# A hybrid encoder layer on one core: filler matmuls around the first transposes and in the choice of tokens are taken out

## What is computed

```python
def hybrid_layer(x, ...):
    h = rmsnorm(x, norm1_g)                       # first step: scale rows, then project
    z = jnp.einsum('bld,dc->blc', h, w_in) + b_in
    ...
    x = x + (g_a * y_a + g_b * y_b) @ w_o
    x = x + expert_choice_moe(rmsnorm(x, norm2_g), router_w, exp_w_gate, exp_w_up, exp_w_down)

def expert_choice_moe(h, router_w, w_gate, w_up, w_down):
    logits = (tok @ router_w).astype(jnp.float32)
    aff = jax.nn.softmax(logits, axis=-1)
    gate, idx = lax.top_k(aff.T, cap)             # cap = 64 tokens per expert and sequence
    xs = tok[idx]                                 # gather
    hid = silu(einsum('ecd,edf->ecf', xs, w_gate)) * einsum('ecd,edf->ecf', xs, w_up)
    ye = einsum('ecf,efd->ecd', hid, w_down) * gate[..., None]
    out = zeros_like(tok).at[idx.reshape(-1)].add(ye.reshape(-1, D))
```

## Time and profile before

| | before |
|---|---|
| median of the runs | 1494.81 us (3 runs, 1494.58 to 1495.61) |
| profiled execution | 1495.38 us, its span 1493.6 us |
| mean granted TensorE clock | 0.994 |
| TensorE busy | 1468.4 us (98%) |
| VectorE, ScalarE, GpSimd busy | 1186.9, 817.8, 163.1 us |

### The profile page before, as it was taken

How to read it: one execution, slowest core, us unless ns; L and a number is a source line. 1 busy time by engine, 2 the same in 40 slices (tenths; PEclk the granted TensorE clock), 3 DMA queues, 4 the chain that set the end, 5 groups by cost and what they waited for, 6 DMA issues and landing times.

```text
span 1493.6 us, 18852 instructions
## 1 busy us (share of the span) xinstructions
PE 1468.4 (98%) x7018; PEld 1234.5 (83%) x7018; DVE 1186.9 (79%) x1016; ACT 817.8 (55%) x771; POOL 163.1 (11%) x119
## 2 busy tenths in 40 slices
PE   9999999999999999998999999999999999999996
PEld 8778888878788888887888888888888888888884
DVE  5688988896667766346888888888888888889896
ACT  6322232223622222333677777778777777777775
POOL 1000001000005200011010111011110112101101
PEclk9999999999999999999999999999999999999998
DMA  7110322533263255677999999999999999999997
GB/s 235 57 43 8 85 77 81 215 93 92 94 226 123 90 180 197 225 252 282 345 363 371 376 377 374 384 374 377 374 372 386 377 375 374 384 375 376 374 360 272
DMA packets 220972, 388.26 MB, mean 260 GB/s; under 512 B 8604, under 2 KB 87772, under 8 KB 220413
## 3 DMA queue, kind: packets, MB, share of 16 engines
q1 hardware_dynamic: 213692, 361.39, 68.2%
q0 software_dynamic: 7232, 26.22, 5.9%
HBM read 348.78 MB, written 38.80 MB: 259 GB/s over the span
## 4 chain that ended last, share of the span: by engine, by line
PE 90%; DVE 6%; DMA 1%; issue 1%; ACT 1%; SPq 0%; POOLq 0%; POOL 0%; DVEq 0%; ACTq 0%
PE ps L1724 29%; PE ps L1726 28%; PE ps L1725 28%; DVE conv_sum L1219 3%; PE ps L2086 1%; DMA w_raw<-in_w_in 1%; PE ps L2078 1%; PE ps L1764 1%; PE ps L2007 1%; DVE w_lo L1185 0%; PE ps L2025 0%; DVE expert_lo L1185 0%; DVE final_rows L1693 0%; PE ps L1731 0%; DVE top_index L1597 0%
## 5 line engine op out<-in xcount | busy, mean ns | idle before, releaser
L1185 DVE TENSOR_TENSOR expert_lo<-expert_raw,expert_hi 128x2048 fp32r<-128x2048 f32 (+1 forms) x285 | 598.5, 2114 | 93.1 <-ACT expert_hi L798 92.1
L798 ACT ACTIVATE expert_hi<-expert_raw 128x2048 fp32r<-128x2048 f32 (+1 forms) x285 | 506.5, 1778 | 177.7 <-PE ps L1726 173.9
L1724 PE MATMUL ps<-expert_hi,slot_tokens_T_hi 128*128 128x512 f32 (+1 forms) x768 | 289.7, 377 | 2.1 <-DVE slot_tokens_T_lo L1185 1.3
L1726 PE MATMUL ps<-expert_hi,slot_tokens_T_lo 128*128 128x512 f32 (+1 forms) x768 | 285.2, 371 | 0.0
L1725 PE MATMUL ps<-expert_lo,slot_tokens_T_hi 128*128 128x512 f32 (+1 forms) x768 | 285.1, 371 | 0.0
L1724 PE MATMUL ps<-hT_hi,w_hi 128*128 128x512 f32 x576 | 227.0, 394 | 1.0 <-DVE hT_lo L1197 1.0
L1726 PE MATMUL ps<-hT_hi,w_lo 128*128 128x512 f32 x576 | 224.3, 389 | 0.0
L1725 PE MATMUL ps<-hT_lo,w_hi 128*128 128x512 f32 x576 | 224.2, 389 | 0.0
L1724 PEld LDWEIGHTS ps<-expert_hi,slot_tokens_T_hi 128*128 128x128 f32 x768 | 144.2, 188 | 25.2 <-issue 3.8
L1726 PEld LDWEIGHTS ps<-expert_hi,slot_tokens_T_lo 128*128 128x128 f32 x768 | 144.2, 188 | 20.4
L1219 DVE SCALAR_TENSOR_TENSOR conv_sum<-a_padded,small_params,conv_sum 128x1024 f32<-128x1024 f32 x120 | 158.1, 1317 | 3.4
(11 more groups left out here) (300 smaller groups left out, 1844.5 us busy)
## 6 DMA issues: line engine op xcount, KB each, us to landing
expert_raw<-in_w_gate SPq DMA_DIRECT2D x64, 1024.0 KB, 8.7
expert_raw<-in_w_up SPq DMA_DIRECT2D x64, 1024.0 KB, 10.1
expert_raw<-in_w_down SPq DMA_DIRECT2D x64, 1024.0 KB, 8.1
expert_raw<-in_w_gate SPq DMA_DIRECT2D x32, 768.0 KB, 7.5
expert_raw<-in_w_up SPq DMA_DIRECT2D x32, 768.0 KB, 6.9
expert_raw<-in_w_down SPq DMA_DIRECT2D x32, 768.0 KB, 8.6
w_raw<-in_w_in SPq DMA_DIRECT2D x36, 512.0 KB, 4.8
gate_in<-gate_spill SPq DMA_DIRECT2D x22, 512.0 KB, 3.8
```

What stands on the lines that cost most here:

```text
L798: nc.scalar.activation(out, src, ACT.Copy, **scale).then_inc(s, 1)
L1185: V.tensor_tensor(out, src, high_part.bitcast(F32), ALU.subtract).then_inc(s, 1)
L1724: nc.tensor.matmul(out, a[0], b[0], start=first, stop=False)
L1726: return nc.tensor.matmul(out, a[1], b[0], start=False, stop=last)
```

## The change

Two helpers and their five calls are taken out of TensorE's program: `warm_up` with 26, 2 and 2 matmuls and the wait for `ones_set` ahead of it, and `keep_busy` with 48 and 22 matmuls. That is 100 matmuls. Nothing else in the kernel is touched; ONES stays, since the layer norm of the convolution branch multiplies by it.

```diff
-            def warm_up(n):
-
-                for _ in range(n):
-                    nc.tensor.matmul(PS[:, XT_BANK[KD - 1], (LT - 1) * P:LT * P], ONES[:], ONES[:], start=True, stop=True)
-
-            pe.wait_ge(ones_set, 1)
-            warm_up(26)
             for t in range(LT):
                 pe.wait_ge(scaled, t + 1)
                 for g in range(KD):
                     mm = x_tile_T(g, t)
                     if t == LT - 1:
                         mm.then_inc(xT_ready, 1)
-                if t < 2:
-                    warm_up(2)
@@
-            def keep_busy(n):
-
-                for _ in range(n):
-                    nc.tensor.matmul(PS[:, 2, 0:P], ONES[:], IDENT, start=True, stop=True)
-
             pe.wait_ge(aff_ready, 1)
             for t in range(HN):
                 mm = nc.tensor.transpose(PS[:, 3, t * P:(t + 1) * P], AFFW[:, t, :], IDENT)
             mm.then_inc(affT_mm, 1)
-            keep_busy(48)
             pe.wait_ge(pair_ready, 1)
@@
-            keep_busy(22)
             tokens_of(0)
             pe.wait_ge(pair_ready, 3)
             pe_body(0, 0, True, False)
```

## The result

The changed kernel takes 1498.49 us (median of 12 runs, 1496.60 to 1499.24), the kernel before on the same chip 1495.51 us (12 runs, 1494.58 to 1496.63): a ratio of 1.0017 with a 95% interval of 1.0010 to 1.0024, so +1.5 to +3.6 us, +3.0 us by the medians. The sign is settled; by size it lies at the 0.2% that I had named as the border of what can be told. The range held it, the forecast of +5.9 us is twice too large.

What follows compares the result with a forecast made beforehand. TensorE, busy in 98% of the span, was taken as the bound, so its losses come out at the end: start +3.6 and middle +2.3 make +5.9 us on 1494.81 us, 1500.7 us, range 1497.1 to 1502.5 us.

Steps and rivals of the forecast that it cites:

- at most some 0.05 us: Fillers' own delay ahead of each of three tiles and the gather's transposes; gain 0 to 0.2 us, taken as 0.
- Rival D: Fillers are on the path and the start's clock is full; 1494.6 or 1497.0 us by the middle's case; chance 0.05.
- clock column's 1.00: At the start, read as no record before the first change; clock taken as half until about 4.7 us.
- The start, forecast +3.6 us: Start without its fillers: late transposes 1.6, cold products 2.3, less 0.3 us for a wait at 20 us.
- The term of the cold products (+2.3 us): Products of x at the start run first at half clock, costing +2.3 us (1.85 to 2.8).
- the late transposes (+1.6 us): Start's transposes of x at half clock, 0.22 us each, make tile 3's first one, and the first product, 1.6 us late.
- Rival B: Transposes lift the clock too: start only +0.9 to +1.6 us, in all 2.6 to 4.6 us; chance 0.33.
- The 1.7 us wait takes nothing up: TensorE's longest wait before 690 us, for VectorE, moves along with TensorE's own z blocks and absorbs no loss.
- The two terms of -0.3 us: The 0.3 us waits at 20 us and for expert_lo in the last stretch each take 0.3 us back.
- The middle, forecast +2.3 us: Choice of tokens and experts: slower transposes +0.3, experts' cold products +2.3, less 0.3 us for the expert_lo wait.
- The slower transposes ahead of them: Slot and gather transposes at half clock, mostly hidden by VectorE's two splits: +0.3 us (0.1 to 0.5).
- upper end of 4.4 us for the start: Top of the start's range in the sum of 4.9 to 7.4 us, beside the middle's 3.0 us.

Runs made afterwards that it cites:

- middle_late: Kernel before with 20 more fillers ahead of the transposes of the first gathered tokens (keep_busy(42) for keep_busy(22)): 1501.29 us, ratio 1.0039.
- transposes_fill: Kernel before with the 70 filler matmuls in the choice of tokens replaced by 140 transposes: 1495.69 against 1495.71 us, ratio 1.0002.
- start_late: Kernel before with 20 more fillers ahead of the first transposes (warm_up(46) for warm_up(26)): 1501.79 us, ratio 1.0035.
- start_late_again: Repeat of the kernel before with warm_up(46) for warm_up(26), 20 more fillers at the start: 1501.61 us, ratio 1.0039.
- no_start: Kernel before without the 30 fillers at the start, the 70 in the choice of tokens kept: 1495.94 against 1496.05 us, ratio 1.0000.
- no_middle: Kernel before without the 70 fillers in the choice of tokens, the 30 at the start kept: 1498.05 us, ratio 1.0015.
- after: The changed kernel, all 100 fillers out, against the kernel before: 1498.49 against 1495.51 us, ratio 1.0017; its profiled execution took 1497.52 us.
- after_again: The changed kernel once more, the second series, against the kernel before on the same chip: 1497.62 against 1495.38 us, ratio 1.0013.
- only_48: Kernel before with keep_busy(22) taken out, keep_busy(48) and the fillers at the start kept: 1498.49 us, ratio 1.0018.
- count_only: Kernel before with keep_busy(48) replaced by 44 fillers and 24 small matmuls of 8 columns: 1504.16 us, ratio 1.0050.

## Why the prediction was right, and where its sum was not

**The path.** That taking the fillers out saves nothing of the 7.80 us that the chain of waits puts down to them was right: with the 52 records gone, the first transposes still start when VectorE has scaled the first tile, at 8.37 us. But "at most some 0.05 us" was too firm. VectorE's scaling of that tile ends at 8.42 us in the kernel before, and the transposes start at 8.65 us, 0.2 us later, behind the last filler; in middle_late it is 1.3 us. In the changed kernel it is 0.05 us. Rival D is dead all the same, since the first product comes later without the fillers and not earlier, and since the clock of the start is not full. That the clock column's 1.00 in the first microseconds stands for no record was right as well: transposes of 421 ns under a shown 1.00 in the changed kernel are those of the earlier trace rows.

**The start, forecast +3.6 us.** This is the step that failed. The term of the cold products (+2.3 us) was zero, since the 32 transposes raised the clock after 4.2 us, and the late transposes (+1.6 us) cost 0.8 us in the pair and 0.4 us on the average of the traces. Rival B had the mechanism right, and even its +0.9 to +1.6 us was too much. I had counted transposes by their records, one where a filler leaves two, and had let the rule of the Trainium skill tip the choice. By the rule that transposes don't engage the full clock (the Trainium skill, "TensorE: Matmul & The Clock Gate", section "Part 4: PE-mode transpose") the clock should not have risen at 12.5 us, nor at 696.9 us under transposes_fill; the traces disagree, and they decide. The record counts agree with the traces: a transpose starts as far behind the last as a filler's record does, 0.11 us at full and 0.21 us at half clock.

**"The 1.7 us wait takes nothing up."** Right for a start that is 5 us late (start_late and start_late_again went through whole). For a loss under 1 us the argument that the wait "moves along" isn't borne out: the wait ends with the landing of one transfer and is 0.6 us shorter on average in the three traces without fillers at the start, and behind it these three aren't late. no_start bounds what reaches the end at +1.2 us, with 0 at its middle.

**The two terms of -0.3 us** failed. The waits for w_lo at 20 us (0.4 us) and for expert_lo in the last stretch (0.3 us) are there in the changed kernel as before. The first belongs to a chain that starts with the same late hT_lo; the second I had not traced to its root.

**The middle, forecast +2.3 us.** Confirmed by no_middle (+2.0 us) and by where the time lies. Its terms: the cold products cost 2.2, 1.7, 1.9 and 2.7 us in the four traces that show them (after, after_again, no_middle, only_48), with the clock down for 4.8, 3.6, 4.1 and 5.8 us behind the first product; I had 1.85 to 2.8 us. The slower transposes ahead of them cost 0 to 0.2 us, as VectorE's splits cover them; I had 0.3 us.

**The sum** by rows is thus 0 to 0.8 us at the start, 2 us in the middle and 0.4 us in the loop, 2.4 to 3.2 us, against the measured 3.0 and 2.2 us; with the traces behind the wait near 321 us it lies nearer to 2.4 us. B is the case that came true, though the second series lies below its 2.6 to 4.6 us. That the stated range holds the result is owed to B's share in it: the forecast's own terms reach no lower than +4.9 us. The upper end of 4.4 us for the start leaves out the term of -0.3 us that the lower end has; with it the forecast's own terms end at 7.1 instead of 7.4 us, which changes nothing here.

## What to carry to other kernels

A filler paid here only where dense work followed a wait in which the clock would have been low, where the fillers reached up to the end of that wait, and where their time at half clock still fitted into it. So each wait on the path needs its own sum, and one of two groups alone can be worth nothing (only_48). Transposes, which an engine often has to do anyway, bring the clock up too, so a warm-up ahead of a run of transposes buys little (here 0.4 us at the first product on average, and nothing that could be shown at the end). And an effect under a microsecond should be followed through the first wait that a transfer sets: there one pair of traces may show it gone, and at the start it may show it twice as large as the average of several.

## What was not expected of the hardware

The clock rose under some 20 transposes (12.5 us, changed kernel) and was held by 44 (transposes_fill), but it fell at 707.4 us under an unbroken run of matmuls with 8 columns, with TensorE 100% busy by the profile (count_only). A busy row is no proof that the clock stays. After a start of steady work the full clock came after 2.5 to about 6 us in these traces: in start_late it rose at 7.0 us, 6.0 us after the first filler, and in no_start at 694.8 us, 2.5 us after the fillers had begun. That made the 48 fillers end early; the clock fell again at 708.5 us with the last 22 already running, and these ended 1.5 us behind the gather's landing. A filler thus has a price of its own in some executions:

```profile
707.10 6.81 PE L2058 MATMUL ps<-small_params,ones 128*128 128x128 f32 x44
713.74 1.04 PE L2074 MATMUL ps<-small_params,slot_tokens 128*128 128x128 f32 x8
```

And 20 matmuls more ahead of the loop made each of its 14 turns 0.1 to 0.2 us longer, while 18 more did not.
